# A decoder step with a routed expert stage: TensorE's outer expert loop set on a fetch block's edge, with a hint for its closing branch

## The reference

```python
g_sel = jnp.argmax(g_logits, axis=-1)                      # one of 4 groups
top_p, top_i = lax.top_k(jax.nn.softmax(e_logits, axis=-1), MOE_TOPK)   # 2 of the group's 8 experts
...
gate = jnp.einsum('td,edf->tef', t, lp['w_exp_gate'])      # 32 experts, 1024 -> 256
up = jnp.einsum('td,edf->tef', t, lp['w_exp_up'])
act = jax.nn.silu(gate) * up * w_tok[..., None].astype(t.dtype)
out = jnp.einsum('tef,efd->td', act, lp['w_exp_down'])     # 256 -> 1024
```

## Time and profile before

| | |
|---|---|
| three runs | 827.18, 827.4 and 831.91 us; median 827.4 us |
| profiled execution | 827.56 us, with a span of 825.8 us |
| TensorE matmuls (PE) | 736.5 us busy, 89% of the span |
| TensorE weight loads (PEld) | 536.2 us busy, 65% |
| VectorE, ScalarE, GpSimd (DVE, ACT, POOL) | 267.2, 192.7 and 98.8 us busy |
| share of the chain of waits by engine | PE 81%, DVE 6%, issue 4%, DMA 4%, ACT 3% |
| mean granted TensorE clock | 0.950 of full speed |
| expert stage on TensorE, first to last matmul of line 538 | 573.3 to 796.7 us |

### The profile page before, as it was taken

The page is one execution under the profiler, slowest core; times in us unless marked ns, Lnnn a source line. Parts: engine busy times, 40 slices in busy tenths (PEclk is TensorE's granted clock), DMA queues, the critical chain, the costliest instruction groups (busy, mean ns, idle before and its releaser), DMA issues.

```text
span 825.8 us, 19442 instructions
## 1 busy us (share of the span) xinstructions
PE 736.5 (89%) x8139; PEld 536.2 (65%) x8140; DVE 267.2 (32%) x742; ACT 192.7 (23%) x496; POOL 98.8 (12%) x232
## 2 busy tenths in 40 slices
PE   5899999999989989898888999874989999989985
PEld 4577777876766666676676777543556656656654
DVE  0226503330133444775671221333211111111122
ACT  1311132123721322121135001330212112211225
POOL 7000000010201303000000000102221212121200
PEclk9799999999999999998898999975999999999997
DMA  9854779898454874800007119754999999999801
GB/s 304 275 159 138 258 258 324 307 323 291 104 153 126 223 198 134 281 26 1 2 2 265 79 46 419 291 232 165 391 410 414 413 413 414 413 414 414 338 15 58
DMA packets 108728, 195.88 MB, mean 237 GB/s; under 512 B 9964, under 2 KB 71097, under 8 KB 100488
## 3 DMA queue, kind: packets, MB, share of 16 engines
q1 hardware_dynamic: 106760, 189.94, 63.8%
q0 software_dynamic: 1920, 5.25, 1.8%
HBM read 185.40 MB, written 9.77 MB: 236 GB/s over the span
## 4 chain that ended last, share of the span: by engine, by line
PE 81%; DVE 6%; issue 4%; DMA 4%; ACT 3%; SPq 1%; POOL 0%; DVEq 0%; POOLq 0%; ACTq 0%
PE ps L1170 16%; PE ps L538 10%; PE ps L1242 7%; PE ps L513 5%; PE ps L551 5%; PE ps L437 4%; PE ps L458 4%; PE ps L514 3%; PE ps L1088 3%; DMA arena<-in_w_in 2%; PE ps L441 2%; PE ps L503 2%; DMA arena<-in_x_sample 1%; PE ps L545 1%; DVE arena L1930 1%
## 5 line engine op out<-in xcount | busy, mean ns | idle before, releaser
L1170 PE MATMUL ps<-arena 128*128 128x288 f32 x576 | 143.5, 408 | 0.9 <-DMA arena<-in_w_in 0.9
L1170 PEld LDWEIGHTS ps<-arena 128*128 128x128 f32 x576 | 108.1, 190 | 31.3 <-DMA arena<-in_w_in 1.3
L538 PE MATMUL ps<-arena 128*32 128x128 f32 x2432 | 86.4, 278 | 15.5 <-issue 13.4
L538 PEld LDWEIGHTS ps<-arena 128*32 128x32 f32 x2432 | 68.9, 111 | 39.7 <-issue 38.5
L1242 PE MATMUL ps<-arena 128*128 128x288 f32 x256 | 75.0, 422 | 5.2 <-ACT arena L1669 3.0
L1242 PEld LDWEIGHTS ps<-arena 128*128 128x128 f32 x256 | 44.6, 191 | 21.1 <-issue 9.6
L513 PE MATMUL ps<-level,arena 32*128 32x256 f32 x624 | 44.8, 401 | 0.5 <-DVE arena L780 0.5
L551 PE MATMUL ps<-arena,hact 128*32 128x256 f32 x608 | 40.7, 385 | 0.0
L775 DVE TENSOR_TENSOR h_row<-h_row,ps 128x64 f32<-128x64 f32 x38 | 8.4, 221 | 96.7 <-ACT h_row L633 96.7
L411 POOL DMA_INDIRECT arena<-h_rows,idx_now x38 | 37.6, 990 | 9.4 <-issue 9.4
L437 PE MATMUL ps<-arena 128*128 128x288 f32 x128 | 35.0, 430 | 0.8 <-ACT arena L1772 0.8
(11 more groups left out here) (441 smaller groups left out, 989.2 us busy)
## 6 DMA issues: line engine op xcount, KB each, us to landing
arena<-in_w_exp_gate SPq DMA_DIRECT2D x32, 1024.0 KB
arena<-in_w_exp_up SPq DMA_DIRECT2D x32, 1024.0 KB
arena<-in_w_exp_down SPq DMA_DIRECT2D x32, 1024.0 KB
arena<-in_w_ada SPq DMA_DIRECT2D x12, 2048.0 KB, 10.1
arena<-in_w_in SPq DMA_DIRECT2D x18, 1024.0 KB, 5.5
arena<-in_w_ada_final SPq DMA_DIRECT2D x4, 2048.0 KB, 14.9
arena<-in_w_in SPq DMA_DIRECT2D x16, 512.0 KB, 4.4
arena<-in_state_ssm_rec SPq DMA_DIRECT2D x8, 512.0 KB, 6.0
```

The lines of the kernel that those rows point to most:

```text
L538: l = mm(ps[CW * q:CW * (q + 1), 5, 0:P].rearrange("p (g f) -> p g f", g=2), xwin[:, at:at + CW], gate_up[:, :, k, f:f + HF], start=(k == ...
L1170: l = mm(ps[:, 2 + 2 * sl + m, 0:TOK], w_ring[sl][:, k, m * P:(m + 1) * P], HN[:, k, :], start=(k == 0), stop=(k == KT - 1))
```

## The change

The outer loop of line 556 is opened through the program's `Fori` in place of the engine's, for TensorE alone, with two more arguments:

```diff
             e.wait_ge(S("tab"), 1)
-            with e.Fori(0, E // ESLOT) as i:
+            with nc.Fori(0, E // ESLOT, engines=[mybir.EngineType.PE], hint_back_edge=True, head_slot={mybir.EngineType.PE: 0}) as i:
                 first = e.value_load(tab[0:1, 0, bass.ds(i * ESLOT, 1)], min_val=0, max_val=MAXWIN)
```

## The result

The changed kernel takes 832.2 us in the median, the kernel before 827.18 in the same series of seven runs each: a ratio of 1.0057, with a 95% interval of 1.0034 to 1.0081 (the ratio is taken from all the runs, here and below, and is not the quotient of the two medians). That is a loss of 4.7 us, and within 1%, as forecast. But the range ended at 831.5, and the forecast was +0.8 us.

The account below looks back on a forecast made before the run. TensorE's own instruction stream was taken to bound the expert stage. Fetch waits 0, hints +0.5 us, entry branch +0.28 and code positions 0 summed to +0.8 us, forecast 828.2 us against the 827.4 median, range 824.4 to 831.5.

Parts of the forecast that it names:

- the gap at a closing is not a fetch: End of each outer-loop pass: thirteen sequencer instructions fill the gap, so fetch waits removed are 0, at most 0.43 us.
- terms 2 and 3: Outer loop: hint 0.12 us in each of 4 passes, 0.5 us; branch over the filling once at entry, 0.28 us.
- term 4: Expert-stage code: new positions inside fetch blocks cost 0, as the windows hide fetching in order.
- second rival: Passes 2 to 4: hint sends the fetcher away, 15 kept blocks are fetched again, 844.7 us; chance 0.07, milder version 0.05.
- mild form: Outer-loop closings: hint loses only the head's block at each, 3 x 1.1 = 3.3 us, 831.5 us; chance 0.05.
- four signs: Outer loop: four hints on line 556, 1.45 to 1.7 us before windows after closings, branch near 216 ns, about 36 packets.
- last sentence of the prediction: Behind the loop: if time leaves the range with lines 538 to 560 unchanged, the code's new place acts there.
- a microsecond at a closing is a microsecond at the end: Expert stage: TensorE's stream sets the pace, so a microsecond between two passes moves the end by about as much.
- first rival: Outer-loop closings: the gap is a fetch after all; the change removes 3.8 us, giving 824.4 us; chance 0.05.

Follow-up runs that it names:

- edge alone: Kernel before, with only the outer loop's first instruction set on a fetch-block edge, no hint: 825.9 us against 827.18, ratio 0.9983.
- one more load: Kernel before, with the load of the pass's first window done twice at the top of each pass: 830.09 us against 826.47, ratio 1.0044.
- written-out version: Kernel before, with the outer loop written out as 32 experts, inner loops kept: 823.82 us against 827.18, ratio 0.9969.
- hint alone: Kernel before, with only the hint at the top of each pass, loop left where it was: 829.89 us against 827.18, ratio 1.0026.
- slots 239 and 100: The change, with the loop starting at slot 239 or 100 of a fetch block: 830.45 us against 827.18 (1.0056) and 827.96 against 826.47 (1.0021).
- three passes: The change, with three loop passes and the last eleven experts written out behind the loop: 833.2 us against 826.47, ratio 1.0081.

## Why the prediction was wrong

**Right: the gap at a closing is not a fetch.** Hint and edge took nothing off it. The edge alone left 216 ns and 1.42 to 1.50 us; one more load lengthened it by 0.61 to 0.72 us, about its own 0.66; without the loop it was gone. The rule in "Runtime: NRT & Kernel Launch" of the Trainium skill, section "Instruction fetch mechanics", by which a target outside a two-page window forces a fetch, does not hold for this loop of six blocks: nothing was fetched at its second and third closing, and the one fetch near the first is that of the block behind the loop. What the same section says of straight code, that crossing a block is mostly hidden, agrees with the 53 fetches of the written-out version.

**Right in kind: terms 2 and 3.** The hint was sized at 0.12 us a pass; the three closings grew by 0.15 to 0.22, because the closing branch also takes 22 to 29 ns more. For the entry I had 0.28 and one hint of 0.12, 0.40 us; its gap grew by 0.56, from 1.68 to 2.24, for the branch over the filling took 407 ns and not at most 236. The rows of line 556 after the change:

```profile
L556 PEldq COMPARE_BRANCH  x5: 87/242/407, 570.1 to 777.5; - x5
L556 PEldq BRANCH_PREFETCH_HINT  x4: 40/42/59, 570.6 to 729.4; - x4
```

**Wrong: term 4**, "New positions of the code inside blocks: 0 ... Fetching code in order is hidden by the windows themselves, wherever a block ends." That was read from the first pass, in which nothing told the fetcher to go elsewhere. I had not asked what the hint takes the place of. The runs show that with a hint the block behind the loop is not fetched in the first pass (change, hint alone, slots 239 and 100, three passes), and without it it is (before, edge alone, one more load). With the edge it is then needed one instruction behind the exit, and the sequencer stands for 4.6 us. In place of the 0 of term 4 the profile has 6.5 us: 4.59 at the exit and 1.95 in the window behind it, at the lower clock.

**Wrong: the second rival's place and price.** It had the mechanism half: the hint sends the fetcher away. But it looked for what is lost inside the loop, in 15 blocks, of which not one was lost (no fetch in passes 2 to 4); and a pass has 6 blocks and not 5, as the six fetches from 565.2 to 604.6 us with the edge alone show. And it priced a late fetch at the packet's own 1.1 us. The runs give 4.6 us for one (2.2 ahead, 1.1, 1.3 behind), 6.2 with DMA saturated, and 1.95 more for the window at the lower clock. One such fetch, at 6.5 us in the profile, is more than the mild form's three at 3.3, and that the measured 832.2 lies close to the mild form's 831.5 is chance.

**The signs looked at the wrong place.** All four signs of being right came about: four hints, 1.62 to 1.67 us at the closings, 238 to 265 ns for the closing branch, 36 packets. They looked at the loop alone. Only the last sentence of the prediction named the place, "somewhere behind the loop"; but it put it down to the new place of the code, and with the edge alone that place costs nothing that is seen.

**Too simple: a microsecond at a closing is a microsecond at the end.** Written out, a closing gives back 0.7 to 0.9 us of its 1.2 to 1.3, for the window behind it grows; lengthened by 0.61 to 0.72 us, it costs 2.2 to 2.4, for the clock falls. So the first rival's 3.8 us for three closings were too much as well: even without a closing, the three give 2.4.

Left open is how the fetcher comes to leave out that block; the runs show only that it does so with the hint. That the remaining loss of the hint alone (1.0000 to 1.0052) is more than its three longer closings could not be told from none.

## What to carry to other kernels

Before helping a branch, look whether it waits: compare its time with that of a short jump, and add up what the sequencer runs in the gap. A hint about where to fetch can have a price at the place where the fetcher would have gone otherwise; here that was the code behind the loop, and where the loop also ended at the end of a block, nothing covered it. So look at the loop's exit too, and not at the closings alone. Where a loop makes few passes, writing it out can be the cheaper cure; here it gained 2.6 us.

## What the runs showed of the hardware that was not expected

An instruction fetch that came late cost far more than its transfer: 4.6 us at the exit, and 6.2 where DMA went on moving 405 to 419 GB/s, for a packet of 1.1 us.

A short pause can cost clock. With one more load, the pauses at the closings are 2.08 to 2.17 us, and behind each of the three the granted clock is 0.50 (615.5 to 618.5, 666.5 to 669.5 and 735 to 738 us). The stretches around the first:

```profile
606.00:615.00 9.00, 6.97 (x122) 4.08 (x122) 1.94 (x5) 2.04 (x7) 2.70 (x6) 1.00 1.01 407
615.00:619.00 4.00, 3.50 (x68) 3.17 (x72) 0.00 (x0) 0.01 (x1) 0.00 (x0) 0.57 1.04 416
619.00:625.00 6.00, 5.64 (x108) 3.60 (x112) 1.12 (x3) 1.25 (x5) 1.35 (x3) 1.00 1.01 414
```

The window from 615.50 on took 6.95 us instead of 5.52 at the same place before, so that a pause longer by 0.7 us cost 2.1 to 2.2; the other two closings did the same (7.09 and 7.10 us, from 5.51 and 5.48). With pauses of 1.45 to 1.67 us, before and after, those windows stayed at 5.48 to 5.52. With slot 100, one pause of 1.65 us did drop the clock (7.11 us), so the length of the pause alone does not decide.
